# LayerNorm of the convolution module: last third's reciprocal root on VectorE and GpSimd, scaling and low parts by turns, last spread moved behind the first product rows

## The reference

```
def layernorm(x, g, b):
    mu = jnp.mean(xf, axis=-1, keepdims=True)
    var = jnp.mean(jnp.square(xf - mu), axis=-1, keepdims=True)
    y = (xf - mu) * lax.rsqrt(var + EPS)
    return (y * g + b)

def conv_module(...):
    ...
    y = causal_dwconv(xp, w_dw, b_dw)
    y = jax.nn.silu(layernorm(y, ln_g, ln_b))
    return y @ w_pw2 + b_pw2, new_buf
```

## Time and profile before

| | us |
|---|---|
| median of 3 runs | 2676.87 |
| lowest and highest run | 2675.86, 2680.51 |
| span of the profiled execution, first to last instruction | 2673.7 |
| TensorE busy in it | 2627.4 (98%) |
| VectorE, GpSimd, ScalarE busy | 2220.9, 1492.9, 960.9 |
| the LayerNorm stage on TensorE, from its first variance product to its first product row | 300.42 to 318.49 |
| the product rows of the stage (144 matmuls) | 318.49 to 343.81 |

### The profile page before, as it was taken

How to read it: one execution, slowest core, us unless ns; L and a number is a source line. 1 busy time by engine, 2 the same in 40 slices (tenths; PEclk the granted TensorE clock), 3 DMA queues, 4 the chain that set the end, 5 groups by cost and what they waited for, 6 DMA issues and landing times.

```text
span 2673.7 us, 44409 instructions
## 1 busy us (share of the span) xinstructions
PE 2627.4 (98%) x17900; PEld 2583.5 (97%) x17900; DVE 2220.9 (83%) x2709; ACT 960.9 (36%) x1589; POOL 1492.9 (56%) x1184
## 2 busy tenths in 40 slices
PE   8999999999999999999999999999999999999998
PEld 8999899999999999999999999989999999999998
DVE  8998668999999898766777777887899999989875
ACT  4001635444444434331221221242544444443433
POOL 5222486777777569862112122117577777765995
PEclk9999999999999999999999999999999999999999
DMA  5222254222222433231111111115411222243231
GB/s 160 56 56 48 48 213 135 75 75 74 75 75 75 190 100 118 67 113 45 49 41 49 41 49 33 49 49 202 142 71 72 75 75 72 72 193 111 83 101 71
DMA packets 154075, 233.92 MB, mean 87 GB/s; under 512 B 69264, under 2 KB 104080, under 8 KB 153872
## 3 DMA queue, kind: packets, MB, share of 16 engines
q1 hardware_dynamic: 81680, 158.36, 17.6%
q10 hardware_dynamic: 72192, 72.73, 8.1%
HBM read 171.86 MB, written 59.20 MB: 86 GB/s over the span
## 4 chain that ended last, share of the span: by engine, by line
PE 89%; DVE 9%; issue 1%; ACT 0%; DMA 0%; POOL 0%; DVEq 0%; ACTq 0%; POOLq 0%
PE BANKS L1281 36%; PE BANKS L1375 13%; PE BANKS L1607 13%; PE BANKS L1241 12%; PE BANKS L1881 3%; PE BANKS L1425 3%; PE BANKS L1663 2%; PE BANKS L1651 1%; PE BANKS L1566 1%; DVE XL L2617 1%; DVE HGA L3242 1%; PE BANKS L1708 1%; DVE XB_B L3084 1%; PE BANKS L1718 1%; DVE BANKS L2705 0%
## 5 line engine op out<-in xcount | busy, mean ns | idle before, releaser
L1281 PE MATMUL BANKS<-XB_A,OPS 128*128 128x288 f32 x3432 | 510.7, 297 | 0.2 <-ACT U L2264 0.2
L1281 PEld LDWEIGHTS BANKS<-XB_A,OPS 128*128 128x128 f32 x3432 | 473.1, 189 | 3.8 <-issue 1.3
L1281 PE MATMUL BANKS<-XB_B,OPS 128*128 128x288 f32 x2904 | 437.0, 296 | 0.0
L996 POOL TENSOR_TENSOR SMALL<-WRAW 128x1 f32<-128x1 f32 x76 | 21.5, 283 | 707.1 <-PE BANKS L1607 455.8
L1281 PEld LDWEIGHTS BANKS<-XB_B,OPS 128*128 128x128 f32 x2904 | 403.8, 189 | 0.0
L3033 DVE SCALAR_TENSOR_TENSOR C<-U,HGA,C 128x1168 f32<-128x1168 f32 x176 | 273.8, 1576 | 35.7 <-ACT C L2283 34.1
L1026 POOL TENSOR_TENSOR OPS<-RAW,OPS 128x512 fp32r<-128x512 f32 x126 | 164.0, 1315 | 199.9 <-ACT OPS L2190 199.9
L1026 POOL TENSOR_TENSOR OPS<-TMP,OPS 128x512 fp32r<-128x512 f32 x168 | 223.2, 1338 | 51.4 <-ACT OPS L2190 51.4
L3105 DVE TENSOR_TENSOR X<-BANKS,X 128x576 f32<-128x576 f32 x224 | 167.8, 750 | 68.2 <-PE BANKS L1375 68.0
L2190 ACT ACTIVATE OPS<-TMP 128x512 fp32r<-128x512 f32 x168 | 106.3, 634 | 283.7 <-POOL TMP L1020 180.3
L999 POOL TENSOR_TENSOR WL<-WRAW,WH 128x1024 fp32r<-128x1024 f32 x76 | 188.4, 2479 | 6.1
(11 more groups left out here) (368 smaller groups left out, 6060.6 us busy)
## 6 DMA issues: line engine op xcount, KB each, us to landing
RAW<-in_w SPq DMA_DIRECT2D x84, 512.0 KB, 4.3
WRAW<-in_w SPq DMA_DIRECT2D x68, 512.0 KB, 3.5
g_kept<-C ACTq DMA_DIRECT2D x44, 512.0 KB, 2.6
x_kept<-X ACTq DMA_DIRECT2D x24, 576.0 KB, 2.8
XB_BF<-x_kept SPq DMA_DIRECT2D x16, 576.0 KB, 8.0
XB_BF<-g_kept SPq DMA_DIRECT2D x32, 288.0 KB, 5.0
WAY_BF<-g_kept SPq DMA_DIRECT2D x32, 288.0 KB, 4.8
WRAW<-in_w SPq DMA_DIRECT2D x32, 256.0 KB, 3.0
```

Source lines behind the costliest of these rows:

```text
L1281: ins = nc.tensor.matmul(out[:, cols], w[:, a, p, :], x[:, b, cols], start=s in OPENS and p == 0 and q == 0, stop=p == PAIRS - 1 and q == ...
```

## The change

- The reciprocal root of the last third no longer comes from ScalarE's Sqrt and VectorE's reciprocal. VectorE reads the three variance columns out of PSUM into R9 as variance / D + eps (`last_variance`, a TENSOR_SCALAR), and GpSimd raises them to the power -1/2 (a TENSOR_TENSOR with `pow` against three columns of -0.5, which a memset at the start fills). Two semaphores, `var_near` and `last_root`, join them. GpSimd's instruction stands between its pair sums and its copies.
- ScalarE loads the Silu table behind the root of the second third, by a one-column Silu, ahead of the last four squares.
- VectorE runs `ln_scaled` and `ln_low` by turns from the first third on, with a lag of three: `ln_low` of (0, 0) stands behind `ln_scaled(0, 3)`. `diagonal(1)` stands behind `ln_scaled(0, 0)`, `last_variance` behind `ln_scaled(0, 4)`, and `diagonal(2)`, without a reciprocal, behind `ln_scaled(0, 7)`; there VectorE also releases the variance banks.
- TensorE's third spread moves behind the rows of k = 6 of the first third, and the idle product ahead of it goes. The rows of the first two thirds wait for the diagonal of their own third (`yd_rdy`); the wait for the release of the variance banks moves ahead of the last third's rows.

```diff
@@ GpSimd
                 nc.gpsimd.tensor_tensor(LSQ[:, 2 * p, :], LSQ[:, 2 * p, :], LSQ[:, 2 * p + 1, :], ALU.add
                                         ).then_inc(pair_rdy, 1)
+            pool.wait_ge(var_near, 1)
+            r = R9[:, (NCH - 1) * NCH:NCH * NCH]
+            nc.gpsimd.tensor_tensor(r, r, MINUS_HALF, ALU.pow).then_inc(last_root, 1)
             for c in range(NCH):
@@ TensorE
             spread_norm(1)
-            idle_products(1, ps_bank(T_PW2 + 1, 2))
-            spread_norm(2)
             idle_products(3, ps_bank(T_PW2 + 1, 2))
             pe.wait_ge(w_split, U_PW2 + 2)
-            free_slot(T_PW2)
...
             for c in range(NCH - 1):
+                pe.wait_ge(yd_rdy, c + 1)
                 for k in range(KD):
                     for j in range(2):
                         ln_row(j, c, k)
+                    if c == 0 and k == KD - 2:
+                        spread_norm(2)
+            free_slot(T_PW2)
@@ ScalarE
                 ln_root(c)
+                if c == NCH - 2:
+                    A(BSUM, EPSC, ACT.Silu)
                 ln_squares(c + 1, KD // 2, KD)
-            ln_root(NCH - 1)
-            act.wait_ge(root_rdy, NCH)
-            act.sem_inc(ps_free[T_VAR % 2], 1)
@@ VectorE
             V.memset(NEG_MEAN, -1.0 / D)
+            V.memset(MINUS_HALF, -0.5)
...
-                dve.wait_ge(root_rdy, c + 1)
                 r = R9[:, c * NCH:(c + 1) * NCH]
-                dc.inc(V.reciprocal(r, r))
-                mine()
+                if c < NCH - 1:
+                    dve.wait_ge(root_rdy, c + 1)
+                    dc.inc(V.reciprocal(r, r))
+                    mine()
+                else:
+                    dve.wait_ge(last_root, 1)
...
-            for k in range(KD):
-                ln_scaled(0, k)
-                if k == 3:
+            def last_variance():
+                dve.wait_ge(var_full, NCH)
+                V.tensor_scalar(R9[:, (NCH - 1) * NCH:NCH * NCH], ps_bank(T_VAR, NCH - 1)[:, 0:CW:P], 1.0 / D, EPS,
+                                ALU.mult, ALU.add).then_inc(var_near, 1)
+            lag = 3
+            for i in range(NCH * KD + lag):
+                if i < NCH * KD:
+                    ln_scaled(i // KD, i % KD)
+                if i == 0:
                     diagonal(1)
-            diagonal(2)
-            for c in range(1, NCH + 1):
-                for k in range(KD):
-                    if c < NCH:
-                        ln_scaled(c, k)
-                    ln_low(c - 1, k)
+                elif i == KD // 2:
+                    last_variance()
+                elif i == KD - 1:
+                    diagonal(2)
+                    dve.sem_inc(ps_free[T_VAR % 2], 1)
+                if i >= lag:
+                    ln_low((i - lag) // KD, (i - lag) % KD)
```

More of the change, by code:

```diff
@@ L225, in build @@
         NEG_MEAN = sb("NEG_MEAN", [P, P])[:]
-        SMALL = sb("SMALL", [P, 3 + 2 * KD + TCH])
+        SMALL = sb("SMALL", [P, 3 + 2 * KD + TCH + NCH])
         EPSC = SMALL[:, 0:1]
@@ L231, in build @@
         PAD = SMALL[:, 1 + 2 * KD + TCH:2 + 2 * KD + TCH]
-        BSUM = SMALL[:, 2 + 2 * KD + TCH:]
+        BSUM = SMALL[:, 2 + 2 * KD + TCH:3 + 2 * KD + TCH]
+        MINUS_HALF = SMALL[:, 3 + 2 * KD + TCH:]
         ARENA_F = 17664
@@ L668, in build @@
         var_full, root_rdy, spread_full = sem("var_full"), sem("root_rdy"), sem("spread_full")
+        var_near, last_root = sem("var_near"), sem("last_root")
         ln_hi, ln_lo = sem("ln_hi"), sem("ln_lo")
```

## The result

The changed kernel takes 2683.38 us (median of 13 runs, 2679.26 to 2688.23), the kernel before 2677.72 us (13 runs beside them, 2675.86 to 2680.51). The ratio is 1.0017, with a 95% interval of 1.0010 to 1.0024: 4.6 us slower by the ratio, 5.7 by the two medians.

A forecast was written before the change was run, and what follows sets the result against it. TensorE, busy 98% of the span, was taken as the bound, with rows waiting for its own program. -2.14 + 1.47 + 0.86 = +0.19 us on a span of 2673.7, plus 3.2 to the median, gave 2677.1 us; range 2674.0 to 2681.0.

The forecast's parts named there:

- the part on other queues: SyncE's weight loads, the release of the variance banks, the memset and ScalarE's missing root: no cost forecast on TensorE.
- rival D: TensorE's gap of some 1.7 us before the rows lowers the clock to 1.2 GHz; 2680 for 3 us; chance 0.04.
- rival C: GpSimd's slow power holds its copy and VectorE's low parts, costing from 1.8 us on; 6 us gives 2681.3; chance 0.06.
- a difference that lies outside this stage: Chance of 0.02 given to the kernel being faster by over 0.2%, from outside the LayerNorm stage.
- The stretch gone: TensorE ahead of the rows: one idle product, the wait and spread 2 go, -2.14 us, first row at 316.35 alone.
- The squares behind the load: ScalarE's table load delays the last four squares; last pair sum ends at 314.35, rows come 1.47 us later.
- The spread among the rows: TensorE's third spread moves among the product rows and costs 0.86 us there, with ends 0.67 and 0.96.
- The first row at 317.82: TensorE's first product row of the LayerNorm stage, 316.35 + 1.47, forecast 0.67 us earlier than before.
- Rival B: ScalarE must run empty ahead of the table load, so squares and rows slide further; 2678.4 or 2678.5; chance 0.08.
- The slack of 1.6 us: Least time by which VectorE's low parts precede their TensorE rows; the power may take 1.8 us before it costs.
- Rival A: ScalarE's table load is free, so its 1.47 us falls to 0 and the time is 2675.6; chance 0.12.
- Rival E: Another item ahead is late, so rows still start at 318.5; +0.86, 2677.7; counted within the forecast's 0.70.

The follow-up runs named there:

- q2: The changed kernel with the memset and the release of the variance banks on GpSimd, so VectorE's instruction count is as before; 2678.01 us, ratio 1.0002.
- e1: The changed kernel with the one-column Silu, and so the table load, behind the last four squares; 2682.07 us, ratio 1.0017.
- e2: The changed kernel with four idle products on TensorE ahead of the third pair of the last variance, filling the gap; 2680.98 us, ratio 1.0014.
- q4: The edits of e2 and q2 together on the changed kernel: gap filled, VectorE's count as before; 2677.73 us, ratio 1.0000.
- q3: q2 with the table load behind the squares as in e1, and the power behind GpSimd's first copy, that of (0, 1); 2676.54 us, ratio 0.9991.
- r1: The kernel before with a VectorE memset at the start cut into two, one more instruction; 2679.83 us, ratio 1.0005.
- r2: The kernel before with a VectorE memset at the start cut into nine, eight more instructions; 2677.42 us, ratio 0.9994.
- q1: The kernel before with a VectorE memset at the start cut into three, two more instructions; 2680.85 us, ratio 1.0015.
- e0: The changed kernel once more, unaltered, for a second trace; one run, 2681.65 us.
- e3: The kernel before with ScalarE held ahead of the last four squares by two copies whose results nobody reads; 2677.66 us, ratio 1.0000.

## Why the prediction was wrong

**The step that failed** is half a sentence at the end of the part on other queues: that "the memset at the start and the missing root of ScalarE cost and give nothing on TensorE". The release of the banks on VectorE was named there, but for its moment, not as an instruction. The two were costed as their own durations, which are hidden. What they do is shift all that follows in VectorE's program, so that at 1775 us a pause of 0.46 us appears there, and two operations of 0.32 and 1.09 us become 1.16 and 2.45: 2.6 us on TensorE in the trace, where the prediction had nothing. None of the rivals had it. The second part of the miss is rival D, 1.44 us, which the sum left at nothing. Together they account for the time: 1.8 us in the stage and 2.6 at 1775 make 4.4, beside 4.6 by the ratio. With the count restored (q2) the time is 2678.01 us and the ratio 1.0002, against the forecast's 2677.1 and +0.2 us.

**The range** was built from this stage's bounds and its upper end, 2681.0, from a power of 6 us, a duration that no row of this case has (0.88 measured; the sum for 6 us in rival C is 2681.3). It had no term for anything outside the stage, though it gave 0.02 to "a difference that lies outside this stage", and that on the faster side alone. The 0.94 for a difference within 0.2% stands, but not by what was reasoned: 0.17% is within it by little, and lies outside the stage for the larger part.

**The sum, term by term.** The stretch gone, -2.14: right, e1's first row is at 316.33 against 316.35 worked out. The squares behind the load, +1.47: right; the load starts 0.02 us behind the root's end, the last pair sum ends at 312.45 + 2.17 = 314.62, or 314.43 without the 0.19 us by which the whole trace was late, against 314.35. Two errors offset each other in that: the four squares follow at 0.41 us, not 0.47 ((1.75 - 0.52) / 3), and the two pair sums take 1.08 us each, not 1.00. The spread among the rows, +0.86: 0.67, the lower of its two ends. The first row at 317.82: right at full clock (317.85 and 317.97 in e2 and q4), wrong in the changed kernel (319.75), which is rival D.

**Rival D, the clock,** had a chance of 0.04 and came true in all three traces of the unfilled stage. Its mechanism and its gap were right (1.7 forecast, 1.76 measured). The evidence against it was one gap of 1.59 us at 19.42 behind which the clock stayed: one row from another stretch of the program, with other work around it, carried too much. Its price was mis-sized: the prediction let each us at the lower level cost up to one, 3 us in all. At half the clock each us loses at most half of one, and 3.4 us at 1.2 GHz cost 1.44. What decides between the gaps that are followed by a low clock and those that are not, no run here shows; the lengths tried are 1.40, 1.59 and 1.76.

**Rival B** (the switch drains ScalarE) is out: 0.02 us between root and load. **Rival C** (slow power) is out as it was put: the power took 0.88 us, inside the ends of 0.2 to 1.32, but over four times the 0.2 that was taken. The slack of 1.6 us was right for rows at 317.82. It is used up when the rows come earlier, which e1 shows: the low part of (0, 1) came at 317.13 + 0.82 = 317.95, and its row was due at about 317.6. **Rival A**'s 2675.6 would not have come about by a free load alone, for that reason; it takes q3's order of power and copy. **Rival E** (the rows don't move) is out: they start at 317.85 at full clock (e2) and at 319.75 in the changed kernel, where it had 318.5.

**What stays open.** Why VectorE pauses where it does: that it pauses for two more instructions and not for one or eight is shown, and the count by 64 (r1 and r2) tells where, but not why, nor why some multiples have no pause. The traces give 2.6 us for pause and held operations, the ratios of q1 and of the changed kernel to q2 some 4 us. The rest may lie in low clocks behind the waits. For it: three of the six traces with held operations have a low clock between 1777 and 1786, and none of the eight without. Against it: the mean granted clock of the timed runs is 0.9965 to 0.9970 in the four kernels with the pause, and 0.9965 to 0.9978 in the others. So this is not shown. The intervals are wide enough to hold both numbers.

## What to carry to other kernels

An instruction off the critical path can cost more than its duration: it moves every later instruction of its engine, and an overlap with another engine that was missed by a tenth of a us can start. When a small change measures slower than its stage explains, add its instructions alone, and take them alone away, before the stage is explained anew. And compare the same instruction all through two traces: the step in the difference names the place.

## What the runs showed of the hardware

- A VectorE operation of two SBUF operands and 96 or 160 columns that started while GpSimd worked on 1024 columns ended 0.1 to 0.2 us behind GpSimd's instruction: 0.25 and 0.32 us became 2.45 and 1.16, in five traces. In a sixth (e0) this held for the first alone: the second, which started 0.02 us behind GpSimd's as in the others, took 0.25, and GpSimd's 2.50 for 2.36. Longer VectorE operations in the LayerNorm stage were slowed much less (0.82 us for 0.54, beside GpSimd's copy).
- A power of 128x3 elements on GpSimd took 0.88 us in the changed kernel and e1, and 1.09 in q3. It is the kernel's only one, so that its first use is in these numbers.
- Behind a gap of 1.76 us on TensorE, with variance products of 128 columns on both sides, the granted clock fell to 1.2 GHz for 3.4 us, beginning 1.2 to 1.5 us after work had started again, in three traces of three. Behind a gap of 1.40 us in the same place it did not, in one trace (e3).
- The place of an instruction in VectorE's program can cost 0.36 us between two dependent operations (0.46 for 0.10). All twelve such pauses of these traces stand in front of a record whose number is a multiple of 64 (320, 1856, 2240), and six waits in front of such a number (640, 896) had none.
